# The first norm of a transformer block taken apart: rows scaled and transposed early, the modulation's factor and shift formed and applied by partition

## The chip, the cores and the metric

The kernel runs on one core of a Trainium2 chip. The metric is the device time of one launch, in microseconds (us). Engines are TensorE (PE, its weight loads are listed as PEld), VectorE (DVE), ScalarE (ACT), GpSimd (POOL) and the queue of SyncE (SP), which issues most transfers.

## The reference, cut to what matters

One block: a modulated norm, two mixers (an RWKV-7 time mix and a sparse attention), a gated merge, a second modulated norm and a mixture of experts. T = 512 tokens, D = 1024. The change is in the first three lines.

```python
cs = jax.nn.silu(c)                                   # c: [1, 1024]
mod = cs @ w_ada[l] + b_ada[l]                        # w_ada: [1024, 6144]
sh1, sc1, gt1, sh2, sc2, gt2 = jnp.split(mod[:, None, :], N_MOD, axis=-1)
u = rmsnorm(h, norm_mix_g[l]) * (1 + sc1) + sh1       # h = x: [512, 1024]
z = u @ w_in[l]                                       # all the projections of both mixers
...
h = h + gt1 * (merged @ w_out[l])
u2 = rmsnorm(h, norm_ffn_g[l]) * (1 + sc2) + sh2
h = h + gt2 * hier_moe(u2, ...)                       # 32 experts, two of them for each token
return rmsnorm(h, norm_final_g)
```

## The kernel before

All of it is one function, written out engine by engine; within an engine the order is that of the code, and semaphores tie the engines together. The first stage forms the modulation and the first norm, and then 44 tiles of projections ("z tiles": weights of `w_in` against `uT`, eight matmuls of 128x128 by 512 columns for most). Later stages are attention, the RWKV scan, merge and second norm, and the experts.

**Transfers.** SP issues them in one order. Weights come in units of 2 MB into a ring of three slots: `ada0` to `ada3` (512 columns of `w_ada` each; 0 and 1 are the shift, 2 and 3 the scale of the first norm), then `zr0`, `zr1`, `ada4`, `zr2` and so on. `ada3` takes the slot of `ada0`, `zr0` that of `ada1`, `zr1` that of `ada2`, `ada4` that of `ada3`. SP waits until a slot is given back before it issues the unit that takes it, and everything behind it in the queue waits too. The order at the start: `c`, `bada` (the bias in rows), `cst` (680 KB of constants), `ada0`, `ada1`, `x` (2 MB), `ada2` and the rest. POOL's own queue brings the norm's gain in `grow`, copied to all 128 partitions (512 KB), and small parameters.

**Modulation.** Rows of `w_ada` lie eight to a partition. For each unit DVE sums them, weighted with silu(c), into `acc` (L627 and seven times L629, each 128x512), and gives the slot back. PE then sums over the partitions with a matrix of ones and adds the bias (`spread_mod`, L784 and L785: two matmuls of 512 columns), so that every partition holds the whole row; ACT copies it out of PSUM to `mod` (L527).

**First norm.** `x` stands with tokens on partitions, in four tiles of 128x1024. ACT squares and sums them (L253), DVE takes the mean (L258), ACT the root (L262). When all of shift and scale is in `mod`, DVE forms the gain (L265) and for each tile the reciprocal (L269), factor and gain (L274) and the shift (L276). PE transposes each tile in eight pieces (L287), ACT copies the pieces to `uT` (L293), and only when all eight copies are done does the first z tile begin (L858 in most of them, L867 for the other orientation).

While the stage runs on, DVE and PE also work off `ada4` to `ada11` between the z tiles; `ada4` is due on DVE with the fifth.

Of the kernel before, what the change touches and what calls it, by code (L numbers as in the profile page):

```python
# [12 lines left out]
P = 128  # L13
D = 1024
T = 512
NT = T // P
# [21 lines left out]
SLOT = 4096  # L38
NEG = -1e30
# [103 lines left out]
def build(nc, A, out):  # L143
# [14 lines left out]
    with ExitStack() as top:  # L158
# [176 lines left out]
        bada = alloc(stage1, "bada", [12, 512])  # L335
        uT = alloc(stage1, "uT", [P, KD, T])
# [4 lines left out]
        grow = misc[:, 0:D]  # L341
        u1 = zrT[:, 8:12, :].rearrange("p (b a) n -> p b (a n)", b=2)
# [28 lines left out]
        def chunks(ap):  # L371
# [13 lines left out]
        n1_square, n1_mean, n1_root, n1_gain, n1_rows, n1_turned, n1_evacuate, _, n1_ev = norm_mod(  # L385
            stage1, "n1", x, u1, uT, grow, junk1, 0, 1, False)
# [38 lines left out]
        with nc.Block() as block:  # L425
            @block.sync
            def _(sp):
                sp.dma_start(crow[:, :], A["c"][0].rearrange("(p k) -> p k", k=KD)).then_inc(s_c, 16)
                sp.dma_start(bada[:, :], A["b_ada"].rearrange("a (u n) -> (a u) n", n=512)).then_inc(s_c, 16)
                sp.dma_start(cst[:, :], A["consts"][:, 0:NC]).then_inc(s_const, 16)  # L430
                load_units(sp, 0, 2)
                sp.dma_start(x, A["x"][0].rearrange("(i p) d -> p i d", p=P)).then_inc(s_h, 16)
                load_units(sp, 2, index["w1k"])
# [12 lines left out]
            def _(pool):  # L446
                link = Chain(pool, w_pool)
                pool.dma_start(grow[:, :], A["norm_mix_g"][0].partition_broadcast(P)).then_inc(s_small, 16)
# [10 lines left out]
                pool.wait_ge(n1_ev, 2 * NT)  # L459
# [16 lines left out]
                pool.wait_ge(s_small, 32)  # L476
# [40 lines left out]
            def _(act):  # L517
# [3 lines left out]
                for i in range(NT):  # L521
                    n1_square(act, i)
                n1_root(act, 0, NT)
                act.wait_ge(s_const, 16)
                for u in range(4):
                    act.wait_ge(s_modp, u + 1)
                    act.activation(mod[:, u // 2, 512 * (u % 2):512 * (u % 2) + 512], ps[:, 4 + u % 2, :],  # L527
                                   ACT.Copy).then_inc(s_mod, 1)
                act.wait_ge(s_parT, 1)
                act.activation(par[:, :], ps[:, 6, 0:34], ACT.Copy).then_inc(s_mod, 1)  # L530
                for i in range(NT):
                    n1_evacuate(act, i)
# [82 lines left out]
            def _(dve):  # L615
# [4 lines left out]
                def ada(u):  # L620
# [7 lines left out]
                    for k in range(1, KD):  # L628
                        link(dve.scalar_tensor_tensor(a, w[:, k, :], csil[:, k:k + 1], a, ALU.mult, ALU.add))  # L629
                    give_back(dve, f"ada{u}")  # L630
                    dve.sem_inc(s_acc, 1)  # L631

                for u in range(4):
                    ada(u)
                    if u == 1:
                        n1_mean(dve, 0, NT)
# [3 lines left out]
                dve.wait_ge(s_small, 32)  # L640
# [1763 lines left out]
```

## Time and profile before

| | |
|---|---|
| median of 3 runs | 1373.03 us (1369.36 to 1373.8) |
| the profiled execution, its own time | 1365.32 us |
| its span, which all rows below count from | 1363.5 us |
| PE busy | 1125.4 us (83%) |
| PE weight loads busy | 566.0 us (42%) |
| DVE busy | 408.0 us (30%) |
| ACT busy | 218.3 us (16%) |
| POOL busy | 164.8 us (12%) |
| first matmul of the projections starts at | 62.48 us |

How to read it: an engine's share is over the whole span, and the stages have different limits, so that what a step is worth is read from its own stretch. In rows of instructions the first two numbers are start and duration in us; "xN" means N instructions one behind the other in that time; the bracket tells how long the engine sat idle before it and what ended that. The shapes of a matmul are stationary rows by columns, then the moving operand; in "ps<-a,b" b is the stationary operand.

### The profile page before, as it was taken

How to read it: one execution, taken by the hardware profiler on the slowest of the kernel's cores; microseconds unless marked ns; L12 is line 12 of the kernel's file. 1: busy time of each engine (PE TensorE's matmuls, PEld its weight loads, DVE VectorE, ACT ScalarE, POOL GpSimd, SP SyncE). 2: the span in 40 equal slices, each digit the busy share in tenths (PEclk: the TensorE clock that was granted, in tenths of full speed). 3: DMA queues.
4: the chain of work that ended last, by engine and by line, in shares of the span. 5: the costliest groups of instructions: out<-in, count | busy, mean ns of one | idle time of the engine just before them, and what ended most of it. 6: DMA issues, size and time to landing. Idle time of an engine off the chain costs nothing. (4 is left out here: it accounts for less than half of the span.)

```text
span 1363.5 us, 16892 instructions
## 1 busy us (share of the span) xinstructions
PE 1125.4 (83%) x7001; PEld 566.0 (42%) x7001; DVE 408.0 (30%) x694; ACT 218.3 (16%) x443; POOL 164.8 (12%) x235
## 2 busy tenths in 40 slices
PE   2699999999997897989799964987778878777880
PEld 0343344544465555979544541332222322222330
DVE  4524436622005444345432444100000010111004
ACT  2101123220003552324200210000000000000002
POOL 1100001124001444223100001000000000000002
PEclk9999999879998997989999976988998998999895
DMA  9512326334324004200174242999999999999985
GB/s 339 212 65 93 123 93 246 125 138 131 105 80 132 1 2 180 78 2 4 70 275 172 106 155 67 429 427 429 429 430 432 431 430 431 430 431 430 430 361 201
DMA packets 61337, 311.73 MB, mean 229 GB/s; under 512 B 6195, under 2 KB 12677, under 8 KB 48729
## 3 DMA queue, kind: packets, MB, share of 16 engines
q1 hardware_dynamic: 49784, 273.79, 50.0%
q0 software_dynamic: 9184, 32.82, 6.3%
q10 hardware_dynamic: 2304, 4.20, 0.8%
q8 instruction: 48, 0.79, 0.2%
q14 instruction: 17, 0.13, 0.0%
HBM read 285.11 MB, written 24.64 MB: 227 GB/s over the span
## 5 line engine op out<-in xcount | busy, mean ns | idle before, releaser
L2299 PE MATMUL ps<-ring,zrT 128*64 128x512 f32 x1024 | 254.5, 655 | 72.4 <-DMA ring<-in_moe_w_gate_dram 32.0
L2299 PEld LDWEIGHTS ps<-ring,zrT 128*64 128x64 f32 x1024 | 83.3, 150 | 232.0 <-issue 200.2
L867 PE MATMUL ps<-ring,uT 128*128 128x512 f32 x384 | 169.8, 599 | 1.2 <-PE ps L867 0.6
L2321 PE MATMUL ps<-ring,mg 128*64 128x512 f32 x512 | 116.8, 610 | 23.4 <-DMA ring<-in_moe_w_down_dram 20.7
L858 PE MATMUL ps<-uT,ring 128*128 128x512 f32 x256 | 113.9, 602 | 1.3 <-ACT uT L293 0.7
L867 PEld LDWEIGHTS ps<-ring,uT 128*128 128x128 f32 x384 | 72.4, 192 | 93.0 <-issue 93.0
L2114 DVE TENSOR_TENSOR zrT<-zrT,ps 128x512 f32<-128x512 f32 x16 | 11.0, 688 | 326.6 <-PE ps L2299 326.6
L1928 ACT ACTIVATE zrT<-ps 128x512 f32<-128x512 f32 x16 | 9.6, 597 | 435.9 <-PE ps L2299 435.9
L2321 PEld LDWEIGHTS ps<-ring,mg 128*64 128x64 f32 x512 | 38.5, 140 | 91.3 <-issue 91.2
L858 PEld LDWEIGHTS ps<-uT,ring 128*128 128x128 f32 x256 | 48.4, 192 | 66.3 <-issue 65.2
L1856 POOL DMA_DIRECT2D y_dram<-zrT x16 | 9.1, 569 | 459.2 <-DVE zrT L2124 459.2
L629 DVE SCALAR_TENSOR_TENSOR acc<-ring,csil,acc 128x512 f32<-128x512 f32 x84 | 63.1, 752 | 3.0
L937 POOL TENSOR_SCALAR prob<-prob,gate,rsum 128x512 f32<-128x512 f32 (+3 forms) x64 | 40.0, 634 | 141.6 <-DVE rsum L991 141.0
L2246 PE MATMUL ps<-ring,uT 128*128 128x512 f32 x128 | 55.8, 594 | 0.7 <-ACT uT L1906 0.7
L2124 DVE TENSOR_TENSOR zrT<-ps,mod 128x512 f32<-128x512 f32 x32 | 22.1, 691 | 114.2 <-PE ps L2321 114.2
L784 PE MATMUL ps<-acc,cst 128*128 128x512 f32 x24 | 18.5, 864 | 32.2 <-DVEq L631 32.2
L1014 ACT ACTIVATE prob<-ps,mx 128x512 f32<-128x512 f32 (+3 forms) x64 | 33.1, 522 | 44.1 <-DVE mx L987 44.0
L987 DVE TENSOR_REDUCE mx<-ps 128x2 f32<-128x1024 f32 (+3 forms) x32 | 26.4, 823 | 36.5 <-PE ps L1068 36.3
L2246 PEld LDWEIGHTS ps<-ring,uT 128*128 128x128 f32 x128 | 24.0, 190 | 29.6 <-issue 28.7
L1081 PE MATMUL ps<-cst,prob 128*128 128x128 f32 x160 | 25.9, 298 | 9.5 <-ACT probT L1026 4.4
L722 DVE TENSOR_TENSOR misc<-misc 128x512 f32<-128x512 f32 x14 | 9.7, 693 | 70.1 <-ACT misc L557 69.7
L1275 POOL TENSOR_TENSOR lm<-ld,late 128x512 f32<-128x512 f32 x20 | 26.1, 1321 | 34.3 <-PE ps L1464 33.7
(355 smaller groups left out, 1278.2 us busy)
## 6 DMA issues: line engine op xcount, KB each, us to landing
ring<-in_moe_w_gate_dram SPq DMA_DIRECT2D x32, 2048.0 KB, 19.1
ring<-in_moe_w_up_dram SPq DMA_DIRECT2D x32, 2048.0 KB, 18.3
ring<-in_moe_w_down_dram SPq DMA_DIRECT2D x32, 2048.0 KB, 19.8
ring<-in_w_ada_dram SPq DMA_DIRECT2D x12, 2048.0 KB, 9.5
ring<-in_w_in_dram SPq DMA_DIRECT2D x9, 2048.0 KB, 13.3
y_dram<-zrT POOLq DMA_DIRECT2D x16, 512.0 KB, 10.5
y_dram<-zeros POOLq DMA_DIRECT2D x1, 7680.0 KB
gates_dram<-gst ACTq DMA_DIRECT2D x16, 256.0 KB, 2.0
```

The costliest lines, as they stand in the source:

```text
L629: link(dve.scalar_tensor_tensor(a, w[:, k, :], csil[:, k:k + 1], a, ALU.mult, ALU.add))
L858: ins = pe.matmul(ps[:, n % 4, :], slot(name, KD, w)[:, k, c0:c0 + P], uT[:, k, :], start=(k == 0), stop=(k == KD - 1))
L867: ins = pe.matmul(ps[:, n % 4, :], uT[:, k, P * i:P * i + P], w, start=(k == 0), stop=(k == KD - 1))
L937: ins = pool.tensor_scalar(p_, p_, gate[:, i, h3:h3 + 1], rsum[:, t % 4, g:g + 1], ALU.mult, ALU.mult)
L987: dve.tensor_reduce(mx[:, t % 4, :], ps[:, 2 * (t % 2):2 * (t % 2) + 2, 0:rows_of(t)], AX, ALU.max, negate=True).then_inc(a_mx, 1)
L1014: ins = act.activation(prob[t % 4][:, g, 0:n], ps[:, 2 * (t % 2) + g, 0:n], ACT.Exp, bias=mx[:, t % 4, g:g + 1], accum_out=rsum[:, t % 4, ...
L1081: ins = pe.transpose(ps[:, 4 + g, P * k:P * k + P], prob[t % 4][:, g, P * k:P * k + P], ident)
L1275: pool.tensor_tensor(lm[q_][:, :, :, :], ld[q_][:, :, :, :], spread8(L8(f"lvl{n}")), ALU.mult)\
L2124: dve.tensor_tensor(yo[:, b % 2, 512 * c:512 * c + 512], ps[:, 2 + c, :], mod[:, 5, 512 * c:512 * c + 512], ALU.mult).then_inc(e_y, 1)
L2246: ins = pe.matmul(ps[:, 4 + n % 3, :], mgT[:, k, P * i:P * i + P], slot(f"wo{k // 4}", 4, D)[:, k % 4, 512 * j:512 * j + 512], start=(k == ...
L2299: ins = pe.matmul(ps[HALF * r:HALF * r + HALF, "gu".index(kind), :], xgT[:, b % 2, k, HALF * r:HALF * r + HALF], w[r][:, k, :], start=(k = ...
L2321: ins = pe.matmul(ps[HALF * r:HALF * r + HALF, 2 + c, :], hdT[:, j, HALF * r:HALF * r + HALF], w[r][:, j, 512 * c:512 * c + 512], start=(j ...
```

## The change

The norm is split at its linear places. The factor of a token (one over its root mean square) is applied to the rows of `x` by POOL as soon as the squares are in, PE transposes those scaled rows while the modulation is still being summed, and ACT copies them to `uT`. The modulation is not spread over all partitions any more: `column_mod` takes the sum over partitions with `acc` as the stationary operand (64 columns with a stride of eight) against a single column of ones, so that factor and shift arrive as one number for each partition and each k. The result is 16 columns of one PSUM bank. DVE adds the bias, forms the gain (`scol`), and applies both to `uT` with one two-operation instruction for each k (L664 of the new kernel); the first z tile's eight matmuls wait for one k each. For `ada3` DVE sums five of the eight rows, and PE takes the other three straight from the weights, with silu(c) as the moving column; PE gives that slot back. `x` comes right behind `ada0`, and `cst` behind `x`. The gain and the bias come as columns (4 KB and 8 KB) where the gain came as 512 KB. The rows of `mod` for shift and scale are no longer written.

```diff
@@ SP @@
                 sp.dma_start(bada[:, :], A["b_ada"].rearrange("a (u n) -> (a u) n", n=512)).then_inc(s_c, 16)
+                load_units(sp, 0, 1)
+                sp.dma_start(x, A["x"][0].rearrange("(i p) d -> p i d", p=P)).then_inc(s_h, 16)
                 sp.dma_start(cst[:, :], A["consts"][:, 0:NC]).then_inc(s_const, 16)
-                load_units(sp, 0, 2)
-                sp.dma_start(x, A["x"][0].rearrange("(i p) d -> p i d", p=P)).then_inc(s_h, 16)
-                load_units(sp, 2, index["w1k"])
+                load_units(sp, 1, index["w1k"])
@@ POOL @@
-                pool.dma_start(grow[:, :], A["norm_mix_g"][0].partition_broadcast(P)).then_inc(s_small, 16)
+                pool.dma_start(gcol[:, :], A["norm_mix_g"][0].rearrange("(p k) -> p k", k=KD)).then_inc(s_small, 16)
+                pool.dma_start(bcol[:, :, :], A["b_ada"][0, 0:2 * D].rearrange("(s p k) -> p s k", s=2, k=KD))\
+                    .then_inc(s_small, 16)
...
-                pool.wait_ge(n1_ev, 2 * NT)
+                pool.wait_ge(x_rs, 1)
+                for i in range(NT):
+                    pool.tensor_scalar(x[:, i, :], x[:, i, :], xrs[:, i:i + 1], None, ALU.mult).then_inc(x_sc, 1)
+                pool.wait_ge(x_ev, 2 * NT)
@@ ACT @@
                 for i in range(NT):
-                    n1_square(act, i)
-                n1_root(act, 0, NT)
+                    if i:
+                        act.wait_ge(x_sq, i)
+                    act.activation(junk1, x[:, i, :], ACT.Square, accum_out=xss[:, i:i + 1]).then_inc(x_sq, 1)
+                act.wait_ge(x_ms, 1)
+                act.activation(xrt, xms, ACT.Sqrt).then_inc(x_rt, 1)
                 act.wait_ge(s_const, 16)
-                for u in range(4):
-                    act.wait_ge(s_modp, u + 1)
-                    act.activation(mod[:, u // 2, 512 * (u % 2):512 * (u % 2) + 512], ps[:, 4 + u % 2, :],
-                                   ACT.Copy).then_inc(s_mod, 1)
+                for n in range(2 * NT):
+                    i, b = n // 2, n % 2
+                    act.wait_ge(x_T, n + 1)
+                    act.activation(uT[:, 4 * b:4 * b + 4, P * i:P * i + P],
+                                   ps[:, n % 4, :].rearrange("p (k t) -> p k t", k=4), ACT.Copy).then_inc(x_ev, 1)
@@ DVE @@
-                    for k in range(1, KD):
+                    for k in range(1, KD - PE_ROWS if u == 3 else KD):
                         link(dve.scalar_tensor_tensor(a, w[:, k, :], csil[:, k:k + 1], a, ALU.mult, ALU.add))
-                    give_back(dve, f"ada{u}")
+                        if u == 1 and k == 3:
+                            dve.wait_ge(x_rt, 1)
+                            dve.reciprocal(xrs, xrt).then_inc(x_rs, 1)
+                    if u != 3:
+                        give_back(dve, f"ada{u}")
                     dve.sem_inc(s_acc, 1)
 
-                for u in range(4):
+                ada(0)
+                dve.wait_ge(x_sq, NT)
+                dve.tensor_scalar(xms, xss, 1.0 / D, 1e-6, ALU.mult, ALU.add).then_inc(x_ms, 1)
+                for u in range(1, 4):
                     ada(u)
...
-                dve.wait_ge(s_mod, 4)
-                n1_gain(dve, link)
-                for i in range(NT):
-                    n1_rows(dve, link, i)
+                dve.wait_ge(s_modp, 4)
+                link(dve.tensor_tensor(scol[:, :, :], ps[:, 4, 0:2 * KD].rearrange("p (s k) -> p s k", s=2), bcol[:, :, :],
+                                       ALU.add))
+                link(dve.scalar_tensor_tensor(scol[:, 1, :], scol[:, 1, :], 1.0, gcol[:, :], ALU.add, ALU.mult))
+                dve.sem_inc(s_mod, 4)
+                dve.wait_ge(x_ev, 2 * NT)
+                for k in range(KD):
+                    dve.tensor_scalar(uT[:, k, :], uT[:, k, :], scol[:, 1, k:k + 1], scol[:, 0, k:k + 1], ALU.mult, ALU.add)\
+                        .then_inc(s_u1, 1)
@@ PE @@
+                def column_mod(u):
+
+                    r = slice(HD * (u % 2), HD * (u % 2) + HD)
+
+                    def column(k, lhs, rhs, first, last):
+                        return pe.matmul(ps[r, 4, KD * (u // 2) + k:KD * (u // 2) + k + 1], lhs, rhs,
+                                         start=(first and u < 2 and k == 0), stop=(last and u >= 2 and k == KD - 1))
+
+                    if u == 3:
+                        need(pe, "ada3")
+                        w = slot("ada3", KD, 512)
+                        for kk in range(KD - PE_ROWS, KD):
+                            for k in range(KD):
+                                column(k, w[:, kk, k::KD], csil[:, kk:kk + 1], False, False)
+                    pe.wait_ge(s_acc, u + 1)
+                    for k in range(KD):
+                        ins = column(k, acc[:, u % 2, k::KD], C("ones")[:, 0:1], True, True)
+                    ins.then_inc(s_modp, 1)
+                    if u == 3:
+                        pe.wait_ge(s_modp, 4)
+                        give_back(pe, "ada3")
...
-                for u in range(4):
-                    spread_mod(u)
+                column_mod(0)
                 pe.wait_ge(s_par, 96)
+                pe.wait_ge(x_sq, NT)
                 pe.transpose(ps[:, 6, 0:34], parr[:, :], C("ident")[0:34, 0:34]).then_inc(s_parT, 1)
-                for i in range(NT):
-                    n1_turned(pe, i)
-                pe.wait_ge(n1_ev, 2 * NT)
-                pe.wait_ge(s_small, 32)
+                for n in range(2 * NT):
+                    i, b = n // 2, n % 2
+                    pe.wait_ge(x_sc, i + 1)
+                    if n >= 4:
+                        pe.wait_ge(x_ev, n - 3)
+                    xv = x[:, i, :].rearrange("t (p k) -> t k p", k=KD)
+                    for k in range(4):
+                        ins = pe.transpose(ps[:, n % 4, P * k:P * k + P], xv[:, 4 * b + k, :], C("ident"))
+                    ins.then_inc(x_T, 1)
+                for u in range(1, 4):
+                    column_mod(u)
+                pe.wait_ge(x_ev, 2 * NT)
+                pe.wait_ge(s_small, 48)
                 pe.wait_ge(s_mod, 5)
                 for n, (kind, name, i, c0) in enumerate(ztiles):
...
                     for k in range(KD):
+                        if n == 0:
+                            pe.wait_ge(s_u1, k + 1)
```

PE, from its first matmul to the z tiles, before. `acc` is the sum of a unit, `zrT` holds `x` here, `ring` the weights.

```order
L784 MATMUL ps<-acc,cst 128x512
L785 MATMUL ps<-bada,cst 128x512
L784 MATMUL ps<-acc,cst 128x512
L785 MATMUL ps<-bada,cst 128x512
L784 MATMUL ps<-acc,cst 128x512
L785 MATMUL ps<-bada,cst 128x512
L784 MATMUL ps<-acc,cst 128x512
L785 MATMUL ps<-bada,cst 128x512
L844 MATMUL ps<-cst,parr 128x34
L287 MATMUL ps<-cst,zrT 128x128 x32
L858 MATMUL ps<-uT,ring 128x512 x56
```

The same place of PE in the changed kernel.

```order
L809 MATMUL ps<-cst,acc 64x1 x8
L882 MATMUL ps<-cst,parr 128x34
L890 MATMUL ps<-cst,zrT 128x128 x32
L809 MATMUL ps<-cst,acc 64x1 x16
L809 MATMUL ps<-csil,ring 64x1 x24
L809 MATMUL ps<-cst,acc 64x1 x8
L907 MATMUL ps<-uT,ring 128x512 x56
```

The 32 transposes have moved ahead of the sums of units 1 to 3, and behind them stand 48 matmuls of one column, 32 of which belong to unit 3.

DVE, from the second unit to the last step of the norm, before (the tiles 1 to 3 repeat the last three rows).

```order
L627 TENSOR_SCALAR acc<-ring,csil 128x512
L629 SCALAR_TENSOR_TENSOR acc<-ring,csil,acc 128x512 x7
L258 TENSOR_SCALAR n_ms<-n_ss 128x4
L627 TENSOR_SCALAR acc<-ring,csil 128x512
L629 SCALAR_TENSOR_TENSOR acc<-ring,csil,acc 128x512 x7
L627 TENSOR_SCALAR acc<-ring,csil 128x512
L629 SCALAR_TENSOR_TENSOR acc<-ring,csil,acc 128x512 x7
L638 CAST ones_bf<-cst 128x128
L639 CAST strict_bf<-cst 128x128
L265 SCALAR_TENSOR_TENSOR misc<-mod,misc 128x1024
L269 RECIPROCAL n_rs<-n_rt 128x1
L274 SCALAR_TENSOR_TENSOR zrT<-zrT,n_rs,misc 128x1024
```

The same place of DVE in the changed kernel, from the middle of the second unit.

```order
L640 SCALAR_TENSOR_TENSOR acc<-ring,csil,acc 128x512 x3
L643 RECIPROCAL n1s<-n1s 128x4
L640 SCALAR_TENSOR_TENSOR acc<-ring,csil,acc 128x512 x4
L638 TENSOR_SCALAR acc<-ring,csil 128x512
L640 SCALAR_TENSOR_TENSOR acc<-ring,csil,acc 128x512 x7
L638 TENSOR_SCALAR acc<-ring,csil 128x512
L640 SCALAR_TENSOR_TENSOR acc<-ring,csil,acc 128x512 x4
L654 CAST ones_bf<-cst 128x128
L655 CAST strict_bf<-cst 128x128
L658 TENSOR_TENSOR scol<-ps,bcol 128x16
L660 SCALAR_TENSOR_TENSOR scol<-scol,gcol 128x8
L664 TENSOR_SCALAR uT<-uT,scol 128x512 x8
```

The reciprocal that releases POOL stands inside the second unit, the last unit is three instructions shorter, and what follows it is two small instructions and eight of 128x512.

## Rows read from the trace of the kernel before

**Rows 1.** Page: idle time ahead of the projections' matmuls, costliest groups.

```profile
L867 PE MATMUL ps<-ring,uT 128*128 128x512 f32 x384 | 169.8, 599 | 1.2 <-PE ps L867 0.6
...
L858 PE MATMUL ps<-uT,ring 128*128 128x512 f32 x256 | 113.9, 602 | 1.3 <-ACT uT L293 0.7
```

**Rows 2.** Waits of SP's queue up to 420 us: for whom, us, times, longest.

```profile
SPq L219 <- PEq L211: 301.6, 10, 48.4
...
SPq L219 <- DVEq L211: 40.9, 6, 9.1
```

**Rows 3.** Timeline of the first 63 us.

```profile
20.81 0.49 DVE L627 TENSOR_SCALAR acc<-ring,csil 128x512 f32<-128x512 f32 x1 [0.25 <-DVE acc L629]
...
25.02 1.03 ACT L253 ACTIVATE ps<-zrT 128x1024 f32<-128x1024 f32 x1 [21.83 <-DMA zrT<-in_x_dram]
...
30.44 0.49 DVE L627 TENSOR_SCALAR acc<-ring,csil 128x512 f32<-128x512 f32 x1 [0.45 <-DMA ring<-in_w_ada_dram]
...
31.36 0.20 ACT L262 ACTIVATE n_rt<-n_ms 128x4 f32<-128x4 f32 x1
...
36.77 0.49 DVE L627 TENSOR_SCALAR acc<-ring,csil 128x512 f32<-128x512 f32 x1 [0.33 <-DVE acc L629]
37.29 5.47 DVE L629 SCALAR_TENSOR_TENSOR acc<-ring,csil,acc 128x512 f32<-128x512 f32 x7
...
47.09 0.60 ACT L527 ACTIVATE mod<-ps 128x512 f32<-128x512 f32 x1 [5.73 <-PE ps L785]
...
61.83 0.60 ACT L293 ACTIVATE uT<-ps 128x512 f32<-128x512 f32 x1 [0.26 <-PE ps L287]
...
62.48 29.16 PE L858 MATMUL ps<-uT,ring 128*128 128x512 f32 x64 [0.69 <-ACT uT L293]
```

**Rows 4.** Windows: engines' busy us, PE clock, DMA share, GB/s.

```profile
21.00:31.00 10.00, 7.89 (x8) 1.83 (x8) 6.25 (x11) 5.52 (x9) 0.00 (x0) 1.00 1.04 394
...
48.00:62.50 14.50, 7.91 (x33) 6.31 (x33) 11.53 (x14) 4.78 (x8) 0.00 (x0) 1.00 0.23 84
```

**Rows 5.** Timeline of POOL near 460 us: multiplication by two scalars, two widths.

```profile
461.00 1.51 POOL L937 TENSOR_SCALAR prob<-prob,gate,rsum 128x512 f32<-128x512 f32 x2 [0.60 <-DVE rsum L991]
462.67 0.87 POOL L937 TENSOR_SCALAR prob<-prob,gate,rsum 128x128 f32<-128x128 f32 x2 [0.16 <-DVE rsum L991]
```

**Rows 6.** Timelines of POOL and of DVE at 538 us, where both read SBUF.

```profile
537.91 1.79 POOL L1275 TENSOR_TENSOR lm<-ld,late 128x512 f32<-128x512 f32 x1
```

```profile
537.88 0.69 DVE L1312 TENSOR_TENSOR xt<-ld,late 128x512 f32<-128x512 f32 x1 [0.78 <-POOL ld L1268]
538.61 1.63 DVE L1313 TENSOR_TENSOR xt<-xt,late 128x512 f32<-128x512 f32 x1
```

**Rows 7.** Timeline of POOL at 559 us: the same instruction with DVE elsewhere.

```profile
559.07 1.27 POOL L1275 TENSOR_TENSOR lm<-ld,late 128x512 f32<-128x512 f32 x1 [4.32 <-PE ps L1464]
```

**Rows 8.** Timelines: PE's matmuls with few moving columns.

```profile
260.74 1.50 PE L861 MATMUL ps<-wgl,uT 128*128 128x24 f32 x12
...
278.76 3.61 PE L861 MATMUL ps<-wgl,uT 128*128 128x24 f32 x16
...
416.37 0.66 PE L825 MATMUL ps<-acc,w 128*64 128x31 f32 x16 [1.81 <-DVE acc L695]
```

**Rows 9.** Groups by shape: DVE instructions of the kinds that the change uses.

```profile
L663 DVE TENSOR_SCALAR misc<-lend,par,omka 128x512 f32<-128x512 f32 x4 | 2.2, 546 | 0.6 <-DVE logp L659 0.2
...
L748 DVE COPY bonus<-ps 128x8 f32<-128x8 f32 x4 | 0.7, 166 | 16.1 <-PE ps L837 15.9 <-DVE acc L629 0.2
```

**Rows 10.** Timeline of PE's weight loads as the projections begin.

```profile
62.48 0.50 PEld L858 LDWEIGHTS ps<-uT,ring 128*128 128x128 f32 x2 [1.09 <-ACT uT L293]
63.50 0.34 PEld L858 LDWEIGHTS ps<-uT,ring 128*128 128x128 f32 x1 [0.52 <-issue]
64.35 0.34 PEld L858 LDWEIGHTS ps<-uT,ring 128*128 128x128 f32 x1 [0.52 <-issue]
...
65.73 0.19 PEld L858 LDWEIGHTS ps<-uT,ring 128*128 128x128 f32 x1 [0.24 <-issue]
```

More of the change, by code:

```diff
@@ L38 @@
 SLOT = 4096
+PE_ROWS = 3
 NEG = -1e30
@@ L335, in build @@
         bada = alloc(stage1, "bada", [12, 512])
+        bcol = alloc(stage1, "bcol", [P, 2, KD])
+        gcol = alloc(stage1, "gcol", [P, KD])
+        scol = alloc(stage1, "scol", [P, 2, KD])
+        n1s = alloc(stage1, "n1s", [P, 4, NT])
         uT = alloc(stage1, "uT", [P, KD, T])
@@ L340, in build @@
         misc = alloc(stage1, "misc", [P, 3 * T + 2])
-        grow = misc[:, 0:D]
-        u1 = zrT[:, 8:12, :].rearrange("p (b a) n -> p b (a n)", b=2)
         zb = misc[:, 0:2 * T + 2].rearrange("p (b t) -> p b t", b=2)
@@ L384, in build @@
         junk1 = ps[:, 6:8, :].rearrange("p b n -> p (b n)")
-        n1_square, n1_mean, n1_root, n1_gain, n1_rows, n1_turned, n1_evacuate, _, n1_ev = norm_mod(
-            stage1, "n1", x, u1, uT, grow, junk1, 0, 1, False)
+        x_sq, x_ms, x_rt, x_rs, x_sc, x_T, x_ev, s_u1 = (sem(f"x_{n}") for n in "sq ms rt rs sc T ev u1".split())
+        xss, xms, xrt, xrs = (n1s[:, n, :] for n in range(4))
         ztiles = [("T", f"zr{t // 4}", t, P * (t % 4)) for t in range(ZT_TILES)]
@@ L475, in _ @@
                 pool.memset(zb[:, :, 0:1], 0.0).then_inc(s_zbz, 1)
-                pool.wait_ge(s_small, 32)
+                pool.wait_ge(s_small, 48)
                 pool.wait_ge(s_par, 96)
@@ L639, in _ @@
                 dve.tensor_copy(strict_bf[:, :], C("strict")).then_inc(s_bf, 1)
-                dve.wait_ge(s_small, 32)
-                dve.wait_ge(s_mod, 4)
-                n1_gain(dve, link)
-                for i in range(NT):
-                    n1_rows(dve, link, i)
+                dve.wait_ge(s_small, 48)
+                dve.wait_ge(s_modp, 4)
[7 more added lines that the diff above has]
+                        .then_inc(s_u1, 1)
                 dve.wait_ge(s_mod, 5)
@@ L777, in spread_mod @@
                     pe.wait_ge(s_acc, u + 1)
-                    if 2 <= u < 4:
-                        pe.wait_ge(s_mod, u - 1)
-                    elif u == 4:
-                        pe.wait_ge(s_mod, 5)
-                    elif u > 4:
-                        pe.wait_ge(s_mod, u)
+                    pe.wait_ge(s_mod, max(u, 5))
                     pe.matmul(ps[:, 4 + u % 2, :], C("ones"), acc[:, u % 2, :], start=True, stop=False)
@@ L839, in side_job @@
                     ins.then_inc(w_job, 1)
-                for u in range(4):
-                    spread_mod(u)
+                column_mod(0)
                 pe.wait_ge(s_par, 96)
+                pe.wait_ge(x_sq, NT)
                 pe.transpose(ps[:, 6, 0:34], parr[:, :], C("ident")[0:34, 0:34]).then_inc(s_parT, 1)
-                for i in range(NT):
-                    n1_turned(pe, i)
-                pe.wait_ge(n1_ev, 2 * NT)
-                pe.wait_ge(s_small, 32)
+                for n in range(2 * NT):
[11 more added lines that the diff above has]
+                pe.wait_ge(s_small, 48)
                 pe.wait_ge(s_mod, 5)
```

3 lines of the change are left out of this document (removed).

## Prediction, made before the changed kernel was run

> **What bounds the kernel now.** I read the idle time ahead of the projections' matmuls first. In two groups of 384 and 256 matmuls PE waited 1.2 and 1.3 us in all [rows 1]: from the first z tile to the end of the projections PE has no gap. Over the same stretch SP's queue waited 301.6 us for PE to give slots back and 40.9 us for DVE [rows 2], so weights wait for PE and not PE for weights. Everything behind is tied to this by semaphores alone. A first z tile that begins earlier therefore moves the rest of the kernel by the same amount, unless a transfer then comes too late.
>
> It begins at 62.48 [rows 3]. The stretch ahead has two parts. Up to about 43 us DMA and DVE both run: the queues move 394 GB/s at a share of 1.04 [rows 4], DVE starts `ada1` at 20.81, `ada2` at 30.44, when it lands, and `ada3` at 36.77, ending at 37.29 + 5.47 = 42.76 [rows 3]. From there nothing is transferred that the first tile needs: the DMA share from 48.0 to 62.5 is 0.23 [rows 4]. It is a serial tail of 62.48 − 42.76 = 19.7 us: the spread of `ada3`, its copy (47.09), four tiles of 1024 columns on DVE, then the last transposes and copies (the last at 61.83) [rows 3]. This tail is what the change attacks.
>
> **The change, part by part.** I follow one chain, with times counted from the start of the span.
>
> *Arrival of `ada1`.* `cst`, `ada0`, `ada1` and `x` had all landed at 25.02 [rows 3]. In the new order `ada1` is the last of the same four. The gain's 0.52 MB are gone, at 394 GB/s [rows 4] 1.3 us, so `ada1` is there at 23.7. `x` lands before it by one unit and `cst`, 2.1 + 0.7 MB or 7.1 us, at about 16.6. ACT then needs from the landing to the root's end 31.56 − 25.02 = 6.5 us [rows 3], of which nothing depends on a unit: root at 23.1, long before the reciprocal that reads it. The squares end before the root, so DVE's new wait for them (behind `ada0`, with `ada1` queued behind it) is over before `ada1` is there: nothing.
>
> *DVE's sums.* A unit takes 36.77 − 30.44 = 6.33 us with the hand-over [rows 3]. `ada1` with a reciprocal (0.2) ends at 23.7 + 6.3 + 0.2 = 30.2, `ada2` at 36.5 (landed at 30.4 − 1.3 = 29.1), and `ada3` has three of its seven steps of 5.47 / 7 = 0.78 us fewer, 5.99 − 2.35 = 3.6 us: 40.1.
>
> *POOL against DVE.* The four multiplications on POOL begin at about 26.9, in the middle of `ada1`, and each reads SBUF, while DVE's steps read two tensors of SBUF. Before shows this pair elsewhere: a DVE step that began while POOL ran took 1.63 us where its neighbour took 0.69, and POOL's took 1.79 [rows 6] where it takes 1.27 with DVE elsewhere [rows 7]. They take turns: POOL's began behind the first DVE step (537.88 + 0.69 = 538.57) and ended at 539.70, and the second DVE step ended 0.54 us after it. POOL at 1024 columns: 0.76 us for 512 and 0.44 for 128 [rows 5], 0.83 ns for each further column, so 1.19. A turn costs 1.05 + 0.6 = 1.65 us where a DVE step alone costs 0.78; four turns cost DVE about 3.1 us less what falls between units. I take 3.1; the ends are 0 and 4 x 1.19 = 4.8. So `ada2` ends at 39.6 and `ada3` at 43.2, and POOL at about 33.6.
>
> The Trainium skill, "SBUF — State Buffer", section Who interferes with whom, says that a DVE instruction with two SBUF inputs and a GpSimd instruction that reads SBUF hold the shared pair of ports for a whole instruction, and that the other fully blocks. By that rule DVE would lose 4.8 us rather than 3.1, and the sum would be 1.7 us later; the rows above agree with the turns but show some overlap of the two.
>
> *Transposes and copies.* 32 and 8 of them, moved under DVE's sums: they follow POOL's tiles and end some 2.5 us after the last, at about 36. On PE they stand ahead of `column_mod(1)`, for which DVE waits before `ada3` (39.9): over by then. The row norm's and gain's work on DVE (four tiles) goes.
>
> *The columns on PE.* Eight for unit 2 (from 39.6), 24 straight from the weights, eight more for unit 3: 40 matmuls of 64 stationary columns and one moving. No row has exactly this. Near it: 16 with 64 stationary columns in 0.66 us, 0.04 each, with two column groups taking turns; 128 stationary columns and 24 moving, 1.50 / 12 = 0.125 at PE's 2.4 GHz level and 3.61 / 16 = 0.226 at the 1.2 GHz level [rows 8]. This place is at 1.2 GHz: the first z matmuls follow at 0.85 us and go over to 0.43 only at 65.7 [rows 10], although the window before reads a granted clock of 1.00 [rows 4]. For half the stationary columns at the slow level I take 0.12, with ends 0.06 and 0.23. Then 39.6 + 32 x 0.12 = 43.4, which is 0.2 behind `ada3`; eight more and 0.3 for the last result: 44.7.
>
> *Factor, shift, first tile.* Two small DVE instructions at 0.17 [rows 9] with their hand-overs, 0.5; the first of eight two-operation steps 0.55 [rows 9]: 45.8. The others follow every 0.55 us, faster than z matmuls at 0.85 [rows 10]: hidden while PE is at its slow level. At the fast level they would pace the first tile, at most 8 x (0.55 − 0.43) = 1.0 us. The two casts (L654, L655) lie under PE's columns: nothing.
>
> *What the ring does.* `zr0` takes `ada1`'s slot at 33 and lies behind `ada3`: in by about 40. `zr1` takes `ada2`'s at 39.6: in by 46, due four tiles after the start, at 60 (64 z matmuls take 29.16 us [rows 3]). `ada4` waits now for PE's hand-back at 44.8, not for DVE at 42.8, and is in at about 51; DVE wants it with the fifth tile, at 64. `zr2` stands behind `ada4` in the queue but waits for `zr0`'s slot anyway. POOL's later transfers come at 36 rather than 62.7, 0.5 MB or 1.3 us among unit loads that have more slack. All nothing, as long as the first tile is not before 40.
>
> The sum: 62.48 − 45.8 = 16.7 us. The profiled execution would go from 1365.32 to 1348.6 and its span from 1363.5 to 1346.8; the median of the three runs is 7.7 us above that execution, and from it the sum gives 1373.0 − 16.7 = **1356.3 us**.
>
> **The rivals.**
> - *POOL costs DVE nothing.* `ada3` ends at 40.1, PE's columns at 41.7, first tile at 42.8: 19.7 us, 1353.3. For it: POOL near 460 us shows no wait [rows 5], though what DVE reads there is mostly PSUM. Against: [rows 6].
> - *POOL is locked for the whole instruction, or comes late.* With 4.8 us lost the result is 1358.0. If DVE instead keeps POOL out until `ada2` is done (36.5), POOL ends at 41.3, transposes at 43, and `column_mod(1)`, behind them on PE, holds back `ada3`: 44 + 3.6, first tile at about 50, 1361. Against: the gap between two DVE steps sufficed at 538.6.
> - *Columns at 0.23 us.* 40 x 0.23 + 0.3 after 39.6 gives 49.1, first tile at 50.2: 12.3 us, 1360.7. For it: all rows with 128 stationary columns at this clock level.
> - *Columns cost what a wide matmul costs, and the kernel gets slower.* If a matmul of one column took as long as one of 512 at this clock level, 0.85 us [rows 10], the 40 would take 34 us, first tile at 75.0, 12.5 us later than now: 1385.5. It decides at (62.48 − 1.1 − 0.3 − 39.6) / 40 = 0.54 us each. Against it: all of [rows 8].
> - *The early start isn't kept.* A transfer comes late, or a later stage has a bound in time of its own: 1373, or something between.
>
> **How the numbers follow.** The forecast with its port contention (1354.5 to 1359) gets 0.52; no contention 0.15; late POOL or slow columns, 1359 to 1362, 0.20; a gain partly lost, 1362 to 1369, 0.05; the start not kept, 0.05; slower 0.03. The range for 8 in 10 takes in the first three: 1351 to 1362, with 1.5 us at the low end for a first tile at the faster clock and for the spread of medians. A measurement of this kernel tells about 0.3% (4 us) from no change: faster by more 0.92, within 0.05, slower 0.03.
>
> **What would show it.** The first 128x512 z matmul at 45 to 47 us, DVE's last step of `ada3` ending near 43, four POOL multiplications of 1.2 to 1.8 us starting near 27 with DVE steps of 1.5 to 1.7 between them, 24 column matmuls within 3 us, and no new idle time before z matmuls later on. Wrong would be: the weights of `zr0` as what ends PE's wait, column matmuls over 0.2 us apart, or a span that shrinks by clearly less than the first tile moved.

## Result and profile after

Over seven runs of each kernel the median went from 1369.36 us (1366.93 to 1373.8) to 1361.58 us (1359.52 to 1365.45). The ratio is 0.9939, with a 95% interval of 0.9918 to 0.9959: the changed kernel is faster by 7.8 us, a little under half of the 16.7 us forecast. The time lies within the range given, 1351 to 1362, by luck: the forecast stood on the median of the first three runs, 1373.0, which was 3.7 us above that of seven. From the median of seven the same range would end at 1358.3, and the result lies above that.

Timeline of the kernel after up to the first z tile; columns: start us, busy us, engine, line, operation, out<-in, form, count, [idle before <- what ended it]. It answers to [rows 3]:

```profile
16.75 1.03 ACT L533 ACTIVATE ps<-zrT 128x1024 f32<-128x1024 f32 x1 [13.18 <-DMA zrT<-in_x_dram]
...
22.75 0.20 ACT L535 ACTIVATE n1s<-n1s 128x4 f32<-128x4 f32 x1
23.83 0.49 DVE L638 TENSOR_SCALAR acc<-ring,csil 128x512 f32<-128x512 f32 x1 [2.18 <-DMA ring<-in_w_ada_dram]
...
26.80 3.82 DVE L640 SCALAR_TENSOR_TENSOR acc<-ring,csil,acc 128x512 f32<-128x512 f32 x4
27.00 12.27 POOL L467 TENSOR_SCALAR zrT<-zrT,n1s 128x1024 f32<-128x1024 f32 x4 [20.18 <-DVE n1s L643]
...
30.95 0.93 DVE L638 TENSOR_SCALAR acc<-ring,csil 128x512 f32<-128x512 f32 x1 [0.33 <-DVE acc L640]
...
31.92 6.95 DVE L640 SCALAR_TENSOR_TENSOR acc<-ring,csil,acc 128x512 f32<-128x512 f32 x7
...
39.32 1.97 PE L890 MATMUL ps<-cst,zrT 128*128 128x128 f32 x8 [1.13 <-POOL zrT L467]
...
43.42 0.49 DVE L638 TENSOR_SCALAR acc<-ring,csil 128x512 f32<-128x512 f32 x1 [4.55 <-PE ps L809]
43.94 3.11 DVE L640 SCALAR_TENSOR_TENSOR acc<-ring,csil,acc 128x512 f32<-128x512 f32 x4
...
49.94 2.06 PE L809 MATMUL ps<-cst,acc 128*64 128x1 f32 x16
...
52.11 0.17 DVE L658 TENSOR_TENSOR scol<-ps,bcol 128x16 f32<-128x16 f32 x1 [4.33 <-PE ps L809]
...
53.34 2.90 PE L907 MATMUL ps<-uT,ring 128*128 128x512 f32 x3 [1.34 <-DVE uT L664]
```

Read it from the bottom. The first z matmul starts at 53.34, where it stood at 62.48: 9.1 us earlier, with 45.8 forecast. PE ran columns without a gap up to 52.0, and DVE, done with `ada3` at 47.05 and with its two casts at 47.78, waited 4.33 us for them. Further up, `ada3` itself started only at 43.42, after 4.55 us in which DVE waited for PE (L809, `column_mod(1)`). This stood behind the transposes of the fourth tile at 39.32, and they waited for POOL, whose four multiplications took 12.27 us. So the chain is POOL, transposes, `column_mod(1)`, `ada3`, columns.

Behind the first tile the gain stays nearly whole. The page's groups that answer to [rows 1] show nearly the same busy time and short waits of PE; of the 1.9 us in the second, 1.3 lie ahead of the very first z matmul:

```profile
L916 PE MATMUL ps<-ring,uT 128*128 128x512 f32 x384 | 170.2, 600 | 1.2 <-PE ps L916 0.6
...
L907 PE MATMUL ps<-uT,ring 128*128 128x512 f32 x256 | 114.8, 606 | 1.9 <-DVE uT L664 1.3
```

The waits of SP's queue up to 420 us (for whom, us, times, longest; [rows 2]) still say that weights wait for PE:

```profile
SPq L220 <- PEq L212: 297.1, 11, 40.7
...
SPq L220 <- DVEq L212: 35.1, 5, 10.7
```

Weight loads of the first z matmuls in the kernel after ([rows 10] for before):

```profile
57.74 0.34 PEld L907 LDWEIGHTS ps<-uT,ring 128*128 128x128 f32 x1 [0.52 <-issue]
58.37 0.19 PEld L907 LDWEIGHTS ps<-uT,ring 128*128 128x128 f32 x1 [0.29 <-issue]
58.80 0.19 PEld L907 LDWEIGHTS ps<-uT,ring 128*128 128x128 f32 x1 [0.24 <-issue]
```

They come every 0.85 us, the pace of the 1.2 GHz level, up to 58.37 and every 0.43 us from there (the granted clock reads 1.00 in both stretches, so that the level has to be read from the pace). That is 5.0 us of the slow pace behind the first matmul, where this profile of before had 65.73 − 62.48 = 3.25. ACT's copy of the first z tile is therefore 8.2 us earlier and not 9.1 (62.86 against 71.08), and the first matmul behind the projections 7.7 us (408.66 against 416.37). This difference does not belong to the change. The kernel before, profiled once more, stayed at the slow pace for 5.1 us too:

```profile
66.81 0.34 PEld L858 LDWEIGHTS ps<-uT,ring 128*128 128x128 f32 x1 [0.52 <-issue]
67.48 0.19 PEld L858 LDWEIGHTS ps<-uT,ring 128*128 128x128 f32 x1 [0.33 <-issue]
67.91 0.19 PEld L858 LDWEIGHTS ps<-uT,ring 128*128 128x128 f32 x1 [0.24 <-issue]
```

Its first z matmul stood at 62.39. The medians differ by 7.8, with an interval of 5.6 to 11.2 us that takes in the whole 9.1.

### The profile page after: what moved, and what is told of

It reads as the page before. It is cut to its first block and busy times, and to the rows that moved or that the text cites. A ratio compares the mean times of both kernels' runs of the same rounds, so it can differ in the third digit from the quotient of the medians.

```text
span 1359.9 us, 17076 instructions
## 1 busy us (share of the span) xinstructions
PE 1122.1 (83%) x7097; PEld 575.0 (42%) x7097; DVE 401.3 (30%) x689; ACT 216.6 (16%) x439; POOL 178.5 (13%) x240
## 3 DMA queue, kind: packets, MB, share of 16 engines
q1 hardware_dynamic: 49784, 273.79, 50.2%
## 5 line engine op out<-in xcount | busy, mean ns | idle before, releaser
L2348 PE MATMUL ps<-ring,zrT 128*64 128x512 f32 x1024 | 251.0, 647 | 73.4 <-DMA ring<-in_moe_w_gate_dram 31.8
L986 POOL TENSOR_SCALAR prob<-prob,gate,rsum 128x512 f32<-128x512 f32 (+3 forms) x64 | 40.1, 637 | 144.5 <-DVE rsum L1040 144.0
L493 POOL TENSOR_TENSOR lend<-bt,lend 128x512 f32<-128x512 f32 x4 | 5.1, 1268 | 206.3 <-DVE mod L688 206.3
L2263 PE MATMUL ps<-ring,zrT 128*128 128x512 f32 x64 | 31.1, 632 | 0.7 <-ACT zrT L1951 0.7
## 6 DMA issues: line engine op xcount, KB each, us to landing
ring<-in_moe_w_gate_dram SPq DMA_DIRECT2D x32, 2048.0 KB, 19.2
```

What stands on the lines that cost most here:

```text
L986: ins = pool.tensor_scalar(p_, p_, gate[:, i, h3:h3 + 1], rsum[:, t % 4, g:g + 1], ALU.mult, ALU.mult)
L2263: ins = pe.matmul(ps[:, 2 * (n % 2) + b, :], yT[:, k, P * i:P * i + P], w[:, k, 512 * j:512 * j + 512], start=(k == 0), stop=(k == 3))
L2348: ins = pe.matmul(ps[HALF * r:HALF * r + HALF, "gu".index(kind), :], xgT[:, b % 2, k, HALF * r:HALF * r + HALF], w[r][:, k, :], start=(k = ...
```

## Experiments

The theory after the result had two parts: POOL's multiplication in this form is slow and comes out late (a), and a column matmul costs 0.23 to 0.26 us rather than 0.12 (b). The rivals were that POOL is held back by DVE's two-input steps, that the width of its instruction matters, and that the 24 columns taken straight from the weights are what is too much. The start of the first z matmul, called z0 below, is the measure: 53.34 in the kernel after. The time of a single profiled run is given beside it, but proves little: seven runs of the kernel after spread over 6 us. z0 itself moves with the transfers, as ACT's first square began anywhere from 16.34 to 17.19 in the runs with the new order, so differences of z0 below half a microsecond say nothing. Diffs are against the kernel after.

**POOL with DVE silent.** The reciprocal comes early, and DVE waits until POOL is done.

```diff
-                        if u == 1 and k == 3:
-                            dve.wait_ge(x_rt, 1)
-                            dve.reciprocal(xrs, xrt).then_inc(x_rs, 1)
...
                 dve.tensor_scalar(xms, xss, 1.0 / D, 1e-6, ALU.mult, ALU.add).then_inc(x_ms, 1)
+                dve.wait_ge(x_rt, 1)
+                dve.reciprocal(xrs, xrt).then_inc(x_rs, 1)
+                dve.wait_ge(x_sc, NT)
```

> The reciprocal stands ahead of unit ada1 and DVE waits there until POOL has scaled all four tiles, so that POOL runs with DVE idle. If POOL's 3.07 us for a tile of 1024 columns come from its turns with DVE, a tile now takes 1.2 us, DVE begins ada1 at about 28.0 and the first z tile starts near 52.4 us of the span. If POOL is slow by itself (2 us or more for a tile), the four take 8 us or more and the first z tile starts at 56 or later. DVE's steps of 128x512 take 0.78 us apart in both.

POOL's row in the timeline:

```profile
23.17 11.31 POOL L467 TENSOR_SCALAR zrT<-zrT,n1s 128x1024 f32<-128x1024 f32 x4 [16.35 <-DVE n1s L649]
```

11.31 / 4 = 2.83 us each with nothing else reading, against 3.07 in company. z0 was 57.71 and the time 1362.41. The instruction is slow by itself, and DVE holds it back by only 0.24 us of the 3.07.

**No scaling at all.** This one leaves the multiplication of the rows out.

```diff
-                for i in range(NT):
-                    pool.tensor_scalar(x[:, i, :], x[:, i, :], xrs[:, i:i + 1], None, ALU.mult).then_inc(x_sc, 1)
+                pool.sem_inc(x_sc, NT)
```

> POOL's multiplication of the rows is left out of the computation (rows of x are transposed unscaled). If late POOL tiles hold back the transposes, behind them column_mod(1), and by it DVE's ada3, then DVE never waits for PE ahead of ada3, which begins at about 36.9, and the columns on PE end the chain: 36.5 + 1.9 + 5.3 + 2.1, first z tile at 47 to 48.5 us instead of 53.3. If POOL's lateness costs nothing because the columns on PE or the weights bound it anyway, the first z tile stays above 52.

DVE's row at the start of `ada3`:

```profile
36.36 0.49 DVE L637 TENSOR_SCALAR acc<-ring,csil 128x512 f32<-128x512 f32 x1 [0.33 <-DVE acc L639]
```

The 4.55 us of waiting are gone and so are the 2.6 us that DVE lost to POOL. z0 was 46.89, the time 1354.3. The first tile comes 1.1 us later than forecast with POOL's price in; the forecast for a POOL that costs nothing was 42.8, so 4.1 us of shortfall are left, and they lie on PE: `ada3` ends at 36.88 + 3.11 = 39.99, as forecast (40.1), and the columns at 43.50 + 2.06 = 45.56, where the forecast had 41.7.

**`column_mod(1)` ahead of the late transposes.**

```diff
                     ins.then_inc(x_T, 1)
-                for u in range(1, 4):
+                    if n == 1:
+                        column_mod(1)
+                for u in range(2, 4):
                     column_mod(u)
```

> On PE column_mod(1) stands behind the first tile's transposes instead of behind all four. DVE then doesn't wait ahead of ada3 (start near 39.2 instead of 43.4, its sum ready at 42.6 instead of 47.0). If PE's columns are what ends last (80 passes at 0.11 us before the last unit's 16), only the 16 passes that left the queue are gained: first z tile at 51.5. If DVE's late sum were the bound, it would come 4.4 us earlier, at 48.9.

DVE starts `ada3` at 39.53 and has it done at 43.2, which is the forecast's figure, but z0 was still 51.40 (1357.92):

```profile
48.00 2.06 PE L809 MATMUL ps<-cst,acc 128*64 128x1 f32 x16
...
51.40 2.90 PE L909 MATMUL ps<-uT,ring 128*128 128x512 f32 x3 [1.34 <-DVE uT L664]
```

With the hold on DVE gone, PE's columns end last. Both causes are real, and they overlap.

**No columns straight from the weights.** `PE_ROWS` 3 became 0, alone and together with the edit before.

```diff
-PE_ROWS = 3
+PE_ROWS = 0
```

> PE takes no rows of ada3 (24 columns fewer on PE), DVE sums all eight (three steps more, 2.35 us). If the 24 columns, 5.3 us on PE behind a queue that is late already, cost what they give back, the first z tile starts within 0.7 us of 53.3 (DVE's sum at 49.4, last columns 2.1, small steps 1.4: 52.9). If they save DVE's 2.35 us as they were meant to, it starts at 55.7.

> column_mod(1) behind the first tile's transposes, and DVE sums all eight rows of ada3. With DVE no longer held, its sum ends at 39.5 + 6.0 = 45.5 and PE, free of the 24 columns, follows with 2.1: first z tile at 49.0, 4.3 us earlier than in the changed kernel, and the time 4 us less than its median (about 0.991 of the kernel before). If the 24 columns on PE had been worth their place, it would be no better than with column_mod(1) moved alone (51.4).

Alone, z0 was 52.59 (one run, 1362.99): the 24 columns save DVE 2.4 us and cost PE 24 x 0.23 = 5.5. Of the 0.75 us by which z0 is earlier, 0.4 come from an earlier landing of `x` (first square at 16.34 against 16.75). From the start of `ada3` to z0 it took 9.6 us, with the 24 columns 9.9: in this order they gain nothing. With `column_mod(1)` early, z0 was 49.23, and over five rounds the median was 1358.83, ratio to before 0.9918 (0.9894 to 0.9941).

**Is it the width or the form of POOL's instruction?** First two halves of 512 columns, then the same product with a second scalar, a one.

```diff
-                    pool.tensor_scalar(x[:, i, :], x[:, i, :], xrs[:, i:i + 1], None, ALU.mult).then_inc(x_sc, 1)
+                    pool.tensor_scalar(x[:, i, 0:512], x[:, i, 0:512], xrs[:, i:i + 1], None, ALU.mult)
+                    pool.tensor_scalar(x[:, i, 512:D], x[:, i, 512:D], xrs[:, i:i + 1], None, ALU.mult).then_inc(x_sc, 1)
```

> POOL scales each tile of 1024 columns in two instructions of 512. With DVE idle an instruction of 1024 took 2.83 us. If the rate of this instruction falls off with its width (0.76 us at 512 columns in the attention stage of the kernel before), eight halves take about 0.8 to 1.1 us each, POOL is done some 3 to 5 us earlier than with 12.3 us for the four tiles, and the first z tile starts 3 us or more earlier, near 50. If the rate belongs to the form of the instruction, eight halves take as long as the four tiles, 12 to 13 us, and the first z tile stays at 53 to 54.

```diff
+                pool.wait_ge(s_const, 16)
                 for i in range(NT):
-                    pool.tensor_scalar(x[:, i, :], x[:, i, :], xrs[:, i:i + 1], None, ALU.mult).then_inc(x_sc, 1)
+                    pool.tensor_scalar(x[:, i, :], x[:, i, :], xrs[:, i:i + 1], C("ones")[:, 0:1], ALU.mult, ALU.mult).then_inc(x_sc, 1)
```

> POOL's instruction has the form that the attention stage uses, two multiplications with a scalar for each partition, here by the factor and by one. If the slow rate belongs to the form with one operation, a tile now takes 1.2 to 1.8 us in DVE's company, POOL is done near 34 and the first z tile starts 3 to 5 us earlier. If not, POOL takes 12 us or more again and the first z tile stays at 53.3.

The halves took 1.55 to 1.97 us each, 14.2 us for all eight, z0 55.34 (1361.55): the width is not it. The two-scalar form, which does more arithmetic, is about twice as fast. The edit adds a second operation and a second scalar at once, and which of them makes the difference stays open. Its timeline:

```profile
26.67 5.54 DVE L641 SCALAR_TENSOR_TENSOR acc<-ring,csil,acc 128x512 f32<-128x512 f32 x4
26.86 6.41 POOL L468 TENSOR_SCALAR zrT<-zrT,n1s,cst 128x1024 f32<-128x1024 f32 x4 [20.05 <-DVE n1s L644]
...
32.54 1.02 DVE L639 TENSOR_SCALAR acc<-ring,csil 128x512 f32<-128x512 f32 x1 [0.33 <-DVE acc L641]
...
39.29 1.72 PE L810 MATMUL ps<-cst,acc 128*64 128x1 f32 x13 [2.79 <-DVEq L647]
39.40 0.49 DVE L639 TENSOR_SCALAR acc<-ring,csil 128x512 f32<-128x512 f32 x1 [0.33 <-DVE acc L641]
...
46.54 2.06 PE L810 MATMUL ps<-cst,acc 128*64 128x1 f32 x16
...
49.93 4.48 PE L908 MATMUL ps<-uT,ring 128*128 128x512 f32 x6 [1.34 <-DVE uT L665]
```

POOL's four take 6.41 us, 1.60 each, and DVE's four steps beside them 5.54 where four take 3.11 alone. All is now about as forecast up to 39.4, and `ada3` ends at 39.92 + 3.11 = 43.03. The 40 column matmuls run from 39.29 to 46.54 + 2.06 = 48.60, which is 9.3 us or 0.23 each. z0 was 49.93, the time 1355.82. This run parts the 7.5 us between forecast and result: 53.34 − 49.93 = 3.4 are POOL's form, and 49.93 − 45.8 = 4.1 the rest, nearly all of it the columns.

**The two-scalar form with DVE silent.** The first experiment's edit with this form of the multiplication:

> POOL scales with the form of two multiplications while DVE waits for it. The forecast's reckoning from the attention stage's widths gives 1.2 us for a tile of 1024 columns (2.83 with the form of one multiplication and DVE idle). Four tiles then take 4.8 us, and the two kernels differ by 6.5 us from there on: first z tile at 51.2 instead of 57.7. If a tile takes 1.6 us here too, as in DVE's company, then what DVE loses isn't given to POOL and the taking of turns is not the mechanism.

```profile
23.04 4.73 POOL L468 TENSOR_SCALAR zrT<-zrT,n1s,cst 128x1024 f32<-128x1024 f32 x4 [16.23 <-DVE n1s L650]
```

4.73 / 4 = 1.18 us each, the 1.19 that the forecast read out of [rows 5]: right for the form in that row, and wrong for the one that the change uses. z0 was 50.98 (1358.36).

**ACT scales the rows.** ACT is idle between root and transposes. The reciprocal comes early, as in the first experiment but without its wait, POOL's loop and its wait go, and of the three rows of weights whose columns PE takes straight one is left.

```diff
-PE_ROWS = 3
+PE_ROWS = 1
...
                 act.activation(xrt, xms, ACT.Sqrt).then_inc(x_rt, 1)
+                act.wait_ge(x_rs, 1)
+                for i in range(NT):
+                    act.activation(x[:, i, :], x[:, i, :], ACT.Copy, scale=xrs[:, i:i + 1]).then_inc(x_sc, 1)
```

> ACT scales the rows instead of POOL (four activations of 1024 columns with a scale for each partition, 1.03 us each as its squares), the reciprocal stands ahead of ada1, and PE takes one row of ada3 instead of three. ACT is done at 27.4, the transposes at 32, DVE is neither slowed nor held: its last sum at 41.6, columns 2.1, first z tile at 45.1. That is 8.2 us earlier than in the changed kernel; if a start that comes earlier is kept to the end, the time is 8 us less than its median, 0.988 of the kernel before. If the gain is lost on the way or a transfer binds (zr0 lands near 40), it is less.

```profile
23.65 4.27 ACT L535 ACTIVATE zrT<-zrT,n1s 128x1024 f32<-128x1024 f32 x4 [0.24 <-DVE n1s L649]
...
37.72 4.69 DVE L640 SCALAR_TENSOR_TENSOR acc<-ring,csil,acc 128x512 f32<-128x512 f32 x6
...
42.52 2.08 PE L808 MATMUL ps<-cst,acc 128*64 128x1 f32 x16 [2.16 <-DVEq L643]
...
45.94 4.61 PE L906 MATMUL ps<-uT,ring 128*128 128x512 f32 x5 [1.34 <-DVE uT L663]
```

ACT needs 1.07 us for each, and all four are done at 27.92, when POOL in the kernel after is still in its first (from 27.00). PE waits 2.16 us for DVE here, as it should: the last eight columns follow the sum at once, and z0 was 45.94. Over five rounds the median was 1356.61 (1354.96 to 1358.4), ratio to before 0.9904 (0.988 to 0.9927), against a median of before of 1369.34. This is the lowest of the three changed kernels that have a median of several runs; the two-scalar form has one run only. The edit joins three things (ACT's scaling, the early reciprocal, fewer rows on PE), and their shares were not measured apart. Its first tile is 7.4 us ahead of that of the kernel after, its median 5.0. The 2.4 us between them are within the two intervals, and stay open.

**The old order of transfers in the changed kernel.**

```diff
-                load_units(sp, 0, 1)
+                sp.dma_start(cst[:, :], A["consts"][:, 0:NC]).then_inc(s_const, 16)
+                load_units(sp, 0, 2)
                 sp.dma_start(x, A["x"][0].rearrange("(i p) d -> p i d", p=P)).then_inc(s_h, 16)
-                sp.dma_start(cst[:, :], A["consts"][:, 0:NC]).then_inc(s_const, 16)
-                load_units(sp, 1, index["w1k"])
+                load_units(sp, 2, index["w1k"])
```

> The order of transfers of the kernel before in the changed kernel: cst, ada0, ada1, x, and so on. x lands at 23.7 instead of 16.7, the squares end at 28.4, and DVE, which waits for them behind ada0, starts ada1 only then instead of at 23.8: 4.7 us later, and all that follows with it, POOL's tiles included: first z tile near 58. If the order of the transfers were worth nothing, it would stay at 53.3.

```profile
23.65 1.03 ACT L533 ACTIVATE ps<-zrT 128x1024 f32<-128x1024 f32 x1 [19.35 <-DMA zrT<-in_x_dram]
```

The rows are squared at 23.65 rather than 16.75, the root comes late, and DVE, which waits for the squares behind `ada0`, starts `ada1` at 28.45. z0 was 57.96 (1366.88). In this kernel the old order costs 4.6 of the 9.1 us. That is not the worth of the order for every arrangement: DVE was done with `ada0` at 19.2 and stood idle for 9.2 us because its wait for the squares lies ahead of `ada1`. The old order with that wait behind `ada1` was not tried, so how the 9.1 us divide between the order and the taking apart of the norm is not shown.

**Where 4 us went between the two spans.** That the span shrinks by clearly less than the first tile moves was one of the signs named for a wrong forecast. The profiled spans differ by 1363.5 − 1359.9 = 3.6 us only, though the first stage ended 7.7 us earlier. I profiled both kernels a second time, unchanged.

> The kernel before, unchanged, profiled once more. If the 3.3 us by which its first profile is shorter than the changed kernel's from the end of the first stage on are chance of one execution (PE's clock falls or stays up at some stage borders), this profile shows stage lengths from the same few steps (attention 115.4 or 117.6, scan 129.8 to 132.4, merge to experts 172 to 177.5) in another mixture, and its stretch from the start of attention to the end is above 943.0, near 947. If they belong to the change, it is 943 again.

> The changed kernel, unchanged, profiled once more. The first z tile starts at 53.3 plus or minus 0.7 again. By chance of one execution the stretch from the start of attention to the end is anywhere from 942 to 951; if the change fixes it, it is 946.2 again with the same stage lengths.

z0 was 62.39 and 53.3, unchanged. But the stretch from the start of the attention to the end of the span took 943.0 and 946.2 us in the two executions of before, and 946.2 and 942.9 in the two of after: the 3 us come and go with the execution and not with the kernel. The sign was there, and it did not mean what I had taken it for. Of the two pairs with like stretches, before against after's second profile differs by 6.5 us in the span and 6.4 at the start of the attention, and before's second against after by 9.1 and 9.2. The windows from the merge to the first expert matmul show one such step. Columns: window, its length, busy us and count of PE, PEld, DVE, ACT and POOL, then granted clock, DMA share and GB/s. Before, its second profile, after, its second profile:

```profile
665.80:839.63 173.83, 139.56 (x439) 73.30 (x439) 69.23 (x165) 18.46 (x37) 8.93 (x14) 0.87 0.41 158
```

```profile
667.97:844.92 176.95, 142.51 (x439) 74.57 (x439) 69.16 (x165) 18.59 (x37) 8.92 (x14) 0.86 0.40 155
```

```profile
659.15:836.24 177.09, 142.36 (x439) 74.72 (x439) 69.14 (x165) 18.68 (x37) 8.94 (x14) 0.86 0.40 155
```

```profile
659.39:831.24 171.85, 137.46 (x438) 71.18 (x439) 69.20 (x165) 18.46 (x37) 8.95 (x14) 0.89 0.42 160
```

DVE, ACT and POOL work the same time in all four. Only PE's busy time moves, by up to 5 us, with the granted clock, 0.86 in the long ones and 0.89 in the shortest. So a change of 4 us can't be read from a pair of spans, but can be from the start of an early stage: z0 agrees within 0.1 us in both pairs. By the start of the attention, 360 us later, the four combinations already give 6.4 to 9.2 us.

## Why the forecast came out as it did

The mechanism held: the early start is kept, and the tail became shorter. Two terms of the sum were mis-sized, and both on the same side, POOL's multiplication and the columns on PE.

- *Arrival of `ada1` at 23.7, `x` before it, root at 23.1.* Measured 23.83, and the root's end 22.95. Right.
- *POOL at 1.19 us alone, 1.65 in turns, done at 33.6.* It began at 27.00 as said and ended at 39.27. This step failed in its size: [rows 5] was a multiplication by two scalars, and I carried its price to a multiplication by one, which takes 2.83 us. It cost 3.4 us of first tile. I had matched the row by engine and width and overlooked its second scalar.
- *DVE loses 3.1 us.* 3.0 with the two-scalar form (5.54 − 3.11 = 2.4 in four steps and 1.02 − 0.49 = 0.5 in the next). With the form of the change 2.6, as 0.71 + 0.44 + 1.48 over the three rows beside POOL. Right in sum, though the sum was not worked out cleanly: four turns of 1.65 us against steps of 0.78 come to 3.5, and 3.1 were taken. The picture of turns fits only the two-scalar form. The Trainium skill, "SBUF — State Buffer", sections SBUF: two separate sides and Who interferes with whom, lets such an instruction hold the ports from start to end: DVE would lose 4 x 1.18 = 4.7 us in the one case and 4 x 2.83 = 11.3 in the other. Neither was seen, so the rival of 1358.0 falls.
- *Transposes end at 36, `column_mod(1)` over before `ada3`.* They ended at 41.3, and `ada3` was held 4.55 us. That is the rival "comes late", with its chain in every step but the first: POOL was not kept out, it was slow.
- *Columns at 0.12 us.* This is the other failed step, and "over 0.2 us apart" was one of the signs named for it. They took 0.23 each in the run where nothing else held them, which is the rival at 0.23, with a first tile of 50.2 forecast and 49.93 measured. It cost nearly all of the remaining 4.1 us. The error lies in the reading: `column_mod(0)` issues eight matmuls, and the trace has two records for each:

```profile
18.43 2.08 PE L809 MATMUL ps<-cst,acc 128*64 128x1 f32 x16 [18.43 <-DMA cst<-consts_dram]
```

 I had taken durations per record from [rows 8] and multiplied them by matmuls of the code. The price per record, 0.13, was close to the 0.12 taken. The transposes, also f32, have one record each (32 for 32), so that there is no rule for all f32. But the trace of before showed the two records, since the code issues L784 once for each unit:

```profile
20.86 2.05 PE L784 MATMUL ps<-acc,cst 128*128 128x512 f32 x2 [20.86 <-DVEq L631]
```

 The z matmuls have two as well: the first z tile's copy comes 8.60 us behind its first matmul, which is about 4 x 0.85 + 12 x 0.43, sixteen records for its eight matmuls. So a z matmul takes 1.7 and 0.86 us where the forecast counts 0.85 and 0.43, and the 64 in 29.16 us are records of 32 matmuls. The weights of the later tiles and `ada4` are thus due later than the forecast says, and eight steps of 0.55 us would not pace the first tile at either level. None of this changed the sum.
- *Last result, small steps and the first tile, 0.3 + 1.1 us.* 1.34, from the end of the columns to z0. Right.
- *What the ring does: nothing late.* Right; no transfer ends a wait of PE's at the first tiles, and the two groups of projection matmuls have as little idle time as before.
- *The slow pace costs both kernels alike.* I didn't name this assumption. Nothing here speaks against it: the slow pace lasted 3.3 and 5.1 us in the two profiles of before, 5.0 and 5.8 in the two of after, and 3.3 with the halves, which have the same row of columns ahead.
- *From chain to median.* The 9.1 us at the first tile lie in the interval of the medians' difference (5.6 to 11.2), so that the early start is kept as far as these runs can tell. The base was 3.7 us high; against the median of seven runs my sum would have given 1352.7, and the result is 8.9 above that. That it lies in the stated range is due to this base. The chance of 0.92 for faster was borne out; of the rivals, the two at 1360.7 and 1361, which I gave 0.20 with all like them, both happened, overlapping to 53.3.

## What to carry to other kernels

Price an instruction from a row of the same form, not only of the same engine and shape: how many scalars and operations it has counts as much as its width. Before multiplying a duration by a count out of the code, check in one loop that the trace's count is the code's. And when a change moves work under the cover of other engines, look for the engine with nothing to do at that moment (here ACT, from 23 us on) before one whose work slows the critical engine, as POOL's cost DVE 2.6 us.

## What the runs showed of the hardware

- A multiplication of 128x1024 f32 on POOL by one scalar per partition takes 2.83 us, with two scalars and two operations (the second by one) 1.18, both with DVE silent. ACT's copy with a scale does the same in 1.07, beside DVE.
- A POOL instruction of the slow form hardly stops DVE: in 12.27 us of POOL beside it, eleven two-input steps of DVE and one single-input step lost 2.6 us in all. The fast form costs DVE 3.0 us in 6.41.
- An f32 matmul with one moving column and 64 stationary ones takes 0.23 us in a dense row, as two records; 128x128 transposes are one record.
- An f32 matmul of 128x512 leaves two records too, 0.85 us each at the 1.2 GHz level and 0.43 at the 2.4 GHz level. The profile's granted clock reads 1.00 in both stretches.
- How long the z matmuls stay at the slow pace differs from execution to execution: 2.7 to 5.9 us over the fourteen profiles, 3.3 and 5.1 with the same kernel before and the same work ahead of them. It is worth up to 1.4 us of a stage's length (8.5 to 10.0 us from z0 to ACT's first copy).
- From one execution to the next of the same kernel the length of the stage from merge to experts moved by 3.1 us (before) and 5.2 us (after), with PE's granted clock from 0.86 to 0.89 and the other engines' work being equal.
